# First chunk of a two-layer encoder: multiplied in plain f32 from the weights as they land, with x scaled by VectorE

## The reference, cut to what matters

```
def rms_norm(x, g):
    xf = x.astype(jnp.float32)
    y = xf * lax.rsqrt(jnp.mean(xf * xf, axis=-1, keepdims=True) + RMS_EPS)
    return y.astype(x.dtype) * g
...
    h = rms_norm(x, pre_g)
    qa, ka, va, ga, qb, kb, vb, gb = _split(h @ w_in, EVEN_IN_WIDTHS)
```

## Time and profile before

| what | us |
|---|---|
| median of the runs | 1176.48 |
| lowest and highest of 3 runs | 1176.21, 1177.12 |
| the profiled execution's own time | 1176.14 |
| span of that execution in the trace | 1174.2 |
| PE busy in the span | 1163.3 |
| VectorE, ScalarE busy | 736.7, 584.1 |

### The profile page before, as it was taken

The page is one execution under the profiler, slowest core; times in us unless marked ns, Lnnn a source line. Parts: engine busy times, 40 slices in busy tenths (PEclk is TensorE's granted clock), DMA queues, the critical chain, the costliest instruction groups (busy, mean ns, idle before and its releaser), DMA issues.

```text
span 1174.2 us, 14646 instructions
## 1 busy us (share of the span) xinstructions
PE 1163.3 (99%) x5476; PEld 972.2 (83%) x5476; DVE 736.7 (63%) x845; ACT 584.1 (50%) x748; POOL 102.9 (9%) x147
## 2 busy tenths in 40 slices
PE   9999999999999999999999999999999999999997
PEld 7888888888888888788888888888888888888886
DVE  6686565666665975754665555565746667668654
ACT  6645454445555654564545444444444444446442
POOL 1000001000000310010100101102011002002100
PEclk9999999999999999999999999999999999999999
DMA  9866676744745784455767666666765656455741
GB/s 360 283 208 222 202 242 198 234 164 143 253 163 229 185 264 179 172 191 181 257 198 238 212 213 217 212 218 203 246 202 177 244 187 229 144 183 179 260 149 72
DMA packets 85816, 244.03 MB, mean 208 GB/s; under 512 B 33264, under 2 KB 50832, under 8 KB 60672
## 3 DMA queue, kind: packets, MB, share of 16 engines
q1 hardware_dynamic: 82416, 234.92, 59.7%
q0 software_dynamic: 2624, 7.75, 1.9%
q10 hardware_dynamic: 720, 0.61, 0.2%
HBM read 220.17 MB, written 8.39 MB: 195 GB/s over the span
## 4 chain that ended last, share of the span: by engine, by line
PE 97%; DVE 1%; ACT 1%; DMA 1%; issue 0%; ACTq 0%; DVEq 0%
PE acc L506 89%; PE bank_x L669 2%; PE bank_y L622 1%; PE bank_x L665 1%; PE bank_y L611 1%; PE bank_x L653 1%; DMA resid<-x_turned 1%; PE bank_y L638 0%; PE bank_x L638 0%; PE bank_y L618 0%; DVE w_lo L1087 0%; DVE mix L1343 0%; PE acc L533 0%; DVE resid L1398 0%; PE acc L539 0%
## 5 line engine op out<-in xcount | busy, mean ns | idle before, releaser
L506 PE MATMUL acc<-w_hi,act_hi 128*128 128x512 f32 x1560 | 615.2, 394 | 0.6 <-DVE w_lo L1087 0.6
L506 PE MATMUL acc<-w_lo,act_hi 128*128 128x512 f32 x1560 | 608.0, 390 | 0.0
L1087 DVE TENSOR_TENSOR w_lo<-raw,w_hi 128x2048 fp32r<-128x2048 f32 x192 | 442.4, 2307 | 176.9 <-ACT w_hi L778 176.7
L778 ACT ACTIVATE w_hi<-raw 128x2048 fp32r<-128x2048 f32 x192 | 367.9, 1916 | 293.3 <-PE acc L506 284.0
L506 PE MATMUL acc<-w_hi,act_lo 128*128 128x512 f32 x1560 | 417.5, 389 | 0.0
L506 PEld LDWEIGHTS acc<-w_hi,act_lo 128*128 128x128 f32 x1560 | 292.8, 188 | 61.9 <-DVE act_lo L1105 0.4
L506 PEld LDWEIGHTS acc<-w_hi,act_hi 128*128 128x128 f32 x1560 | 293.2, 188 | 58.5 <-DVE w_lo L1087 1.1
L506 PEld LDWEIGHTS acc<-w_lo,act_hi 128*128 128x128 f32 x1560 | 293.2, 188 | 57.1
L785 ACT ACTIVATE unit<-acc,pre_r 128x512 f32<-128x512 f32 x78 | 49.5, 686 | 125.4 <-PE acc L506 122.2
L443 POOL TENSOR_TENSOR rope_c<-unit,cst 128x256 f32<-128x256 f32 (+1 forms) x19 | 14.1, 742 | 747.7 <-ACT unit L785 596.1
L1246 DVE TENSOR_SCALAR mix<-bank_x 128x256 f32<-128x256 f32 (+1 forms) x24 | 10.1, 423 | 65.7 <-PE bank_x L669 65.7
(11 more groups left out here) (181 smaller groups left out, 616.5 us busy)
## 6 DMA issues: line engine op xcount, KB each, us to landing
raw<-weights SPq DMA_DIRECT2D x192, 1024.0 KB, 5.0
qk_raw<-postg SPq DMA_DIRECT2D x176, 64.0 KB, 2.0
p_moved<-p_blocks SPq DMA_DIRECT2D x16, 256.0 KB, 5.6
probs<-p_moved SPq DMA_DIRECT2D x64, 64.0 KB, 1.9
raw<-weights SPq DMA_DIRECT2D x7, 512.0 KB, 9.3
postg<-post_g POOLq DMA_DIRECT2D x2, 1024.0 KB, 8.2
resid<-x_perm POOLq DMA_DIRECT2D x2, 1024.0 KB, 8.8
p_moved<-p_blocks SPq DMA_DIRECT2D x16, 128.0 KB, 5.0
```

The costliest lines, as they stand in the source:

```text
L506: m = nc.tensor.matmul(tiles[t][:, :], a[:, kt, t * P:(t + 1) * P], w[:, buf, kk * NB:(kk + 1) * NB], start=(kt == 0 and a is act_hi and w ...
L778: nc.scalar.activation(w_hi[:, at % SPLIT, :], raw[:, at % RAW, :], ACT.Copy).then_inc(S["hi_ready"], 1)
L1087: nc.vector.tensor_tensor(w_lo[:, at % SPLIT, :], raw[:, at % RAW, :], w_hi[:, at % SPLIT, :].bitcast(F32), ALU.subtract).then_inc(S["lo_r ...
```

## The change

- Chunk 0 is no longer split. PE multiplies it in plain f32, eight matmuls of 512 columns, straight from `raw` as each piece lands.
- x times the gain for these products is made by VectorE in plain f32 (`x_scaled`, laid in the first block of `unit`, which is free then). The rounded x of tiles 0 to 3 (`act_hi`, `act_lo`) is still made, since later column blocks use it.
- x tiles 0, 1 and 2 to 3 move from ScalarE's queue to SP's, each ahead of its piece of weights. The gain is then the only transfer that ScalarE issues at the start.
- The counts of `hi_ready` and `lo_ready` for chunk 0 are kept up by ScalarE's warm-up instruction and by a small memset.
- Since PE now reads `raw` itself, SP's load of chunk 4 waits until PE has finished chunk 0 (`chunk_used`).

```
# SP
-            for n, cols in enumerate(PIECES):
+            for n, (cols, k) in enumerate(zip(PIECES, (slice(0, 1), slice(1, 2), slice(2, 4)))):
+                sp.dma_start(xT[:, k, :], x_turned[:, k, :]).then_inc(x_first[n], 16)
                 sp.dma_start(raw[:, 0, cols], weights[0][:, cols]).then_inc((w_first + landed)[n], 16)
...
+                if isinstance(i, int) and at + BODY * i == RAW:
+                    sp.wait_ge(S["chunk_used"], 1)
                 sp.wait_ge(S["lo_ready"], at + BODY * i - RAW + 1)
# PE
-                pair = (2 * half, 2 * half + 1)
-                for kt in pair:
-                    pe.wait_ge(S["x_hi"], kt + 1)
-                    for w, part in ((w_hi, "hi"), (w_lo, "lo")):
...
-                pe.wait_ge(S["turn_taken"], half + 1)
-                for kt in pair:
+                for kt in (2 * half, 2 * half + 1):
+                    pe.wait_ge((w_first + landed)[min(kt, 2)], 16)
+                    pe.wait_ge(S["first_x"], kt + 1)
                     for t in range(NT):
-                        m = nc.tensor.matmul(acc[0][t][:, :], act_lo[:, kt, t * P:(t + 1) * P],
-                                             w_hi[:, 0, kt * NB:(kt + 1) * NB], start=False, stop=False)
+                        m = nc.tensor.matmul(acc[0][t][:, :], x_scaled[:, kt, t * P:(t + 1) * P],
+                                             raw[:, 0, kt * NB:(kt + 1) * NB], start=(kt == 0), stop=False)
# ScalarE
-            act.dma_start(xT[:, 0, :], x_turned[:, 0, :]).then_inc(x_first[0], 16)
             act.dma_start(preg[:, :, :], pre_g).then_inc(S["preg_in"], 16)
             act.wait_ge(S["o_full"], CREDIT)
-            nc.scalar.activation(warm[:, :], credit[:, 0:1], ACT.Copy)
-            for kt in (1,):
-                act.dma_start(xT[:, kt, :], x_turned[:, kt, :]).then_inc(x_first[kt], 16)
-            act.dma_start(xT[:, 2:4, :], x_turned[:, 2:4, :]).then_inc(x_first[2], 16)
+            nc.scalar.activation(warm[:, :], credit[:, 0:1], ACT.Copy).then_inc(S["hi_ready"], 1)
...
-                act.wait_ge((w_first + landed)[min(kt, 2)], 16)
-                nc.scalar.activation(w_hi[:, 0, kt * NB:(kt + 1) * NB], raw[:, 0, kt * NB:(kt + 1) * NB], ACT.Copy).then_inc(
-                    S["first_hi" if kt < CK - 1 else "hi_ready"], 1)
# VectorE
+            nc.vector.memset(spare[:, :], 0.0).then_inc(S["lo_ready"], 1)
...
+            dve.wait_ge(S["preg_in"], 16)
             for kt in range(CK):
-                cols = slice(kt * NB, (kt + 1) * NB)
-                dve.wait_ge(S["first_hi" if kt < CK - 1 else "hi_ready"], kt + 1 if kt < CK - 1 else 1)
-                nc.vector.tensor_tensor(w_lo[:, 0, cols], raw[:, 0, cols], w_hi[:, 0, cols].bitcast(F32),
-                                        ALU.subtract).then_inc(S["first_lo" if kt < CK - 1 else "lo_ready"], 1)
+                dve.wait_ge(x_first[min(kt, 2)], 16)
+                nc.vector.tensor_scalar(x_scaled[:, kt, :], xT[:, kt, :], preg[:, 0, kt:kt + 1], None,
+                                        ALU.mult).then_inc(S["first_x"], 1)
                 dve.wait_ge(S["x_hi"], kt + 1)
                 m = nc.vector.scalar_tensor_tensor(act_lo[:, kt, :], xT[:, kt, :], preg[:, 0, kt:kt + 1],
```

More of the change, by code:

```diff
@@ L206, in build @@
         warm = sb("warm", [P, 1])
+        spare = sb("spare", [P, 1])
         std = sb("std", [P, NT])
@@ L228, in build @@
         xT = resid[:, :, :].rearrange("p t (k n) -> p (t k) n", n=SEQ)
+        x_scaled = unit[:, 0, :, :].rearrange("p t (k n) -> p (t k) n", n=SEQ)
         squares = [unit[:, blk, :, :].rearrange("p t n -> p (t n)") for blk in range(3)] + [
@@ L248, in build @@
         names = ("ident_in consts_in preg_in vecs_in resid_in postg_in out_sent "
-                 "x_hi half_hi half_lo first_hi first_lo warm_in ones_in row_sums row_full hi_ready lo_ready chunk_used tile_done proj_ready roped rope_a "
+                 "x_hi half_hi half_lo first_x warm_in ones_in row_sums row_full hi_ready lo_ready chunk_used tile_done proj_ready roped rope_a "
                  "mix_turned sp_moved1 sp_moved0 pool_moved1 pool_moved0 turn_full turn_hi turn_taken qk_turned qk_in qk_hi qk_ready k_full k_split k_ready g_ready "
```

## The result

| what | before | after |
|---|---|---|
| median of 20 runs each, us | 1176.20 | 1178.06 |
| lowest and highest, us | 1175.14, 1178.14 | 1177.31, 1181.65 |
| the profiled execution's own time, us | 1176.14 | 1177.76 |
| its span, us | 1174.2 | 1176.0 |

The ratio is 1.0016, with a 95% interval from 1.001 to 1.0023: the change makes the kernel slower by some 1.9 us. The forecast was 1176.4.

A forecast was written before the change was run, and what follows sets the result against it. Behind PE's 99% it saw VectorE's reductions after chunk 5's weights land holding the sum of the squares: 0 of 1.8 us arrives, minus 0.1 from the front, 1176.14 to 1176.0, on the median 1176.4 us; range 1174.6 to 1178.3.

The forecast's parts named there:

- x moved to SP's queue: Step on the first transfers: three more issues on SP, bounded by 0.2 us gain and 0.45 loss, taken as 0.1 gain.
- They don't run dry: Claim that weights of chunks 1 to 3, issued 1.35 us later, still keep the transfers supplied until 20.0 us.
- front worse by over 1 us: Rival: the first loads run one after another, giving 1177.5 us; chance 0.05, shared with a front better by as much.
- Chunk 1 starts at 13.5: Step: PE begins chunk 1 at 13.5 instead of 15.3 us, 1.8 us earlier, its second half landing at 11.5.
- a sign of being wrong: Listed sign against the forecast: chunk 1 starting after 15.6 us.
- VectorE still delivers its last sum at 42.67: Step: VectorE's last reduction ends unchanged, so PE waits 2.0 us instead of 0.26 and sums at 42.78.
- holds nothing that the change touches: Claim on the 14.21 us chain from chunk 5's weights landing through ScalarE's split and VectorE's reductions to PE's sum.
- The gate: PE's sum of the squares after chunk 5 waits for VectorE's reductions, so 0 of 1.8 us arrives; full-clock chance 0.50.
- PE is the bound throughout: Rival: PE limits the whole kernel, so the full 2.1 us arrives, 1174.4 us; chance 0.08.
- The clock rival: Strongest rival: PE's wait before the sum of the squares drops the clock, costing up to 1.7 us, 1178.1; chance 0.31.
- The price of a plain f32 matmul: Step for chunk 0: 0.89 us per 512-column matmul, 7.1 us for the eight.
- half rate: Rival: chunk 0's plain f32 matmuls run at the warm-up's pace, 14.2 us, giving 1181.1 us; chance 0.06.

The follow-up runs named there:

- e2: the kernel before with only x tiles 0 to 3 moved to SP's queue, splits of chunk 0 kept; 1178.72 us, ratio 1.0016.
- e1: the changed kernel with x tiles 0 to 3 back on ScalarE's queue, plain f32 products kept; 1177.08 us, ratio 1.0.
- e4: the changed kernel with x back on ScalarE's queue and the sum of the squares taken one chunk later; 1175.67 us, ratio 0.9989.
- e11: e4 with 14 warm-up matmuls instead of 10; 1174.41 us, ratio 0.998 against the kernel before.
- e9: the changed kernel with each piece of weights issued ahead of its x on SP's queue; 1177.38 us, ratio 1.0011.
- e3: the changed kernel with twelve small unused matmuls on zeros added behind chunk 0 to fill PE's pause; 1178.71 us, ratio 1.0017.
- e10: e1 with the gain ahead of x on ScalarE's queue; 1176.77 us, ratio 1.0004.
- e8: the changed kernel with chunk 0's x and weights mixed on both SP's and ScalarE's queues; 1176.45 us, ratio 1.0001.
- e7: the changed kernel with all of chunk 0's x first on SP's queue, then its weights, not alternating; 1177.55 us, ratio 1.001.
- e12: e5 with 16 warm-up matmuls instead of 10; 1175.02 us, ratio 0.9987.
- e5: the kernel before with only the sum of the squares taken one chunk later; 1175.26 us, ratio 0.9994.

## Why the prediction was wrong

**The step that failed is "x moved to SP's queue".** It was priced at between 0.2 us of gain and 0.45 of loss, and 0.1 of gain was taken, "since the engines are full in all rows after 5.6". Measured, the second half of chunk 1 landed 2.3 us later and chunk 5's split started 1.2 us later; e2 shows that this part alone does it, and e1 that the rest without it does not. Two rows should have widened the bound. In the kernel before, the DMA share was 1.06 from 8 to 9 us and yet only 311 GB/s were moved: a full share is not a full rate. And the engines were *not* full before 5.6 us (0.72, 211 GB/s), which is just where the change moves transfers. The step saw that chunks 1 to 3 would be issued 1.35 us later and put that at nothing ("They don't run dry"), as if the bytes would land in the order and at the rate of the kernel before. The rival for it (front worse by over 1 us, 1177.5) had the right place and was given 0.05.

**"Chunk 1 starts at 13.5" falls with it:** 15.78, past the 15.6 that the prediction had named as a sign of being wrong. ScalarE took the split and the roundings in the time forecast (13.87 to 15.73), from a landing 2.3 us later.

**"VectorE still delivers its last sum at 42.67"** had the right mechanism on a wrong premise. The chain "holds nothing that the change touches", but it begins when chunk 5 lands, and that moved: 43.88.

**The gate was right.** In e1, where the front is that of before, PE stood 1.68 us where 2.0 were forecast, the sum began at 43.02 against 42.78, and the median did not change. The rival "PE is the bound throughout" falls: the 1.2 us by which PE started earlier were spent waiting. e4 and e11 take the gate away, and PE passes without a wait. What that alone is worth in time is not clear of the noise (e1 1.0 [0.9991, 1.0009], e4 0.9989 [0.998, 0.9998]).

**The clock rival was right in kind and wrong in place.** Its time, 1178.1, lies beside the measured 1178.06, but by another road: in the changed kernel PE never stood at the gate (28.94 us of matmuls hid the reductions), and the clock fell at the wait ahead of chunk 1. At the gate it is seen in the experiments. The profiles with a wait there of 0.26 (before), 0.28 (e9), 0.34 (e3) and 0.59 us (e10) held 1.00; those with 1.26 (e8), 1.31 (e7), 1.68 (e1) and 2.22 us (e2) had 0.50 within some 2 us of the end of the wait. The Trainium skill (Perfetto Trace Analysis, Matmul Optimizations) asks for matmuls back to back because the engine scales its power with use; these eight rows agree. The length of a wait does not decide alone, though: ahead of chunk 1 PE stood 1.75 us in e7 and 1.46 us in e2, and both held 1.00 (rows of e7):

```profile
15.64 0.50 PE L513 MATMUL acc<-w_hi,act_hi 128*128 128x512 f32 x1 [1.75 <-ACT act_hi L888]
...
15.49:18.90 3.41, 3.26 (x14) 2.73 (x15) 2.91 (x6) 2.52 (x5) 0.00 (x0) 1.00 1.04 405
```

**The price of a plain f32 matmul was right:** two records of 0.43 us, 6.9 us for the eight (3.60 + 3.70 = 7.3 with the ends of the two groups), forecast 7.1. The rival "half rate" was not seen in the changed kernel; e4's profile shows its price, 0.85 us a record. The scaling of x took 0.35 us, as forecast.

**A smaller miss the other way:** chunk 0 began at 5.40, not 6.0. With the queue to itself, the gain was in at 3.16, not at 6.14 - 0.45. This was hidden, as the prediction said anything ahead of the gate would be.

What stays open: why 16 DMA engines move 0.75 MB less in the first 14 us when one queue carries what two carried (4.31 against 3.56 MB), and why e8 lies between. That the move of x to SP's queue is the cause is shown. What it does is not: the later issue, the sharing of one queue, or both.

## What to carry to other kernels

Price a transfer that changes queues by the rate that the stretch reaches, in MB moved by a certain time, and not only by the issues that it adds; a two-way test (the move alone, the rest alone) settles it in two runs. Ahead of a gate that another engine sets, an earlier start is worth nothing until the gate is moved, and every wait that it makes can cost clock behind it. Move the gate first, then look at what the faster start is worth: here 0.6 us, with a longer warm-up in both kernels.

## What was not expected of the hardware

- **One queue against two at the start.** With x on SP's queue, 171 to 237 GB/s were moved between 3 and 6 us; with x on ScalarE's, 258 to 301; with both mixed on two queues (e8), 178. The Trainium skill (DMA: Bandwidth & Descriptors, Issuing engines are not separate DMA queues) has it that issuing from several engines saves only the sequencer's time, which is usually small. Here that time was not small: chunk 1's second half was issued 1.6 us later. And it was not all: from issue to landing it took 0.7 us more, and in e8, issued as early as before, 1.0 us more (9.39 against 8.4). The measurement decides.
- **A share of 0.94 at 290 GB/s.** From 9.06 to 12.47 the changed kernel's DMA engines were nearly always busy and yet moved a quarter less than before (402). Busy engines are not evidence of full rate.
- **With a longer warm-up the runs lie closer.** e11 spans 0.6 us over eleven runs and e12 0.8; e4 and e5, with ten warm-up matmuls, 2.2 and 2.6. The two pairs are of two batches; the kernel before spans 3.5 us in the first pair's and 3.1 in the second's.
